# Mixer 1 of a two-block transformer kernel: when its attention starts, and what stands between its steps

## The chip, the cores and the metric

The kernel runs on one core of a Trainium2 chip. The metric is the device time of one launch, in microseconds (us). TensorE does the matrix products, VectorE and ScalarE the elementwise work, GpSimd (POOL in the profile) a few small things, and SyncE issues the loads of weights. A tensor engine bank is one of eight PSUM banks of 512 columns.

## The reference, cut to what matters

The reference is two transformer blocks on 256 tokens of width 1024. The change lies in the first block's second part, the mixer:

```
x = x + 0.5 * gate * swiglu(modulate(x))          # first FFN, "f1"
h = modulate(x, norm_w, shift, scale)             # shift, scale: parts of silu(c) @ w_ada + b_ada
proj = h @ w_in                                   # c_q 256, c_kv 128, k_rope 32, conv 3*512, gates 2*1024
q  = rms_norm(c_q) @ w_uq                         # 8 heads of 64 + 32 (rope)
kv = rms_norm(c_kv) @ w_ukv                       # 8 heads of 64 (key) + 64 (value)
q, k: rms_norm per head, rope on the last 32; k_rope is shared by all heads
o_attn = causal softmax(q k^T * scale) v
o_conv = gate_b * conv3(gate_c * xv)
y = (sum over branches of sigmoid(gates) * (branch @ w_branch)) @ w_out
x = x + gate * y                                  # then the second FFN, "f2", with its own shift and scale
```

The modulation `silu(c) @ w_ada + b_ada` gives 72 columns of 128 values; f2's shift is columns 48 to 55 and its scale columns 56 to 63.

## The kernel before, in words

All activations stand transposed, features on the 128 partitions and 256 tokens along the free dimension. Every fp32 operand is split in two fp32r halves, hi and lo, and a product is three matmuls: hi x hi, hi x lo, lo x hi. A **tile** is one 128 x 128 block of weights, so three matmuls; `Plan.tiles` counts them from the kernel's start, and tile numbers here and below are that count.

Weights come in **units** of up to 2048 columns through a raw buffer of four slots (`load`, SyncE). ScalarE copies a unit to the ring as **hi** (two halves of up to 1024 columns) and VectorE subtracts to get **lo** (two pieces). A unit of modulation weights is two **ada** pieces of VectorE (L209) and needs no hi. A load can be issued when the unit four before it has been used up by its pieces. `take_unit` issues the hi and puts the pieces in a list, `pend`. A piece leaves the list (`piece`) at three kinds of place: `fill()` calls in the code, every 4 tiles when more than two are pending (`went`), and when a unit's first tile is due (`need`: units are taken three ahead, and not more than three pieces may be pending when one is taken). With `self.hold` set the first two do nothing. With `self.apart` set, `take_unit` issues only the first half of hi, and the second half is issued just ahead of the unit's first lo. Unit w33 is the first of mixer 1; w37 holds the queries' weights, w46 those of gates 1.

The order of the work is written out once, in `Plan`, and each engine runs its own steps in that order, strictly one behind the other. In mixer 1 the groups of projections follow `M1_ORDER`: c_q and c_kv (tile 528), conv_in 1 (552), conv_in 0 (568), queries and keys (584), conv_out 0 (604), conv_in 2, conv_in 3, conv_out 2 (652), then gates 1 (668), gates 2 (684), gates 0 (700), and five more groups of gates, each 16 tiles, to tile 796; then the branches and the output projection. Each group has two banks and is evacuated when it is done: for gates, VectorE's `gate_in` twice, then ScalarE's `gate_shift` and `gate_tanh` twice.

Beside them, `in_tiles(n, ...)` starts things n tiles behind tile 604: `heads(0)` and `heads(1)` (scaling and rope of the queries of each half of the tokens, VectorE), `head_keys` (scaling of the keys on VectorE, and a copy of the rope keys to all heads on ScalarE, `heads_kr`), and the **attention**, a generator that is moved on by one step whenever the tile count passes a multiple of 3.5. Its first move does nothing. Its steps are: eight times four transposes of two heads' queries or keys (`turn_heads`, TensorE, L227) with a copy out on ScalarE (`turned_heads`), in banks B0 and B3 by turns, so that the third turn needs the first one's copy done; then in half steps for n = 0, 1, ...: scores of head n (B0 or B3), `masked_1` (VectorE), `exp_1` (ScalarE); turn of P of head n - 2 (bank B1 alone, so it needs the copy out of the turn before it, `turned_1`, ScalarE); the product of P and V for a pair of heads (B7) every other step; and half a step later `between(n)`: `normal_1`, the scaling of head n by its sums (VectorE), and the split of a finished pair into hi and lo (`o_hi_1`, `o_lo_1`).

Before the change the first head turn is at tile 679, the first scores at 707. In ScalarE's order the first two `turned_heads` (tiles 679, 683) stand ahead of the evacuation of gates 1 (684). Two ada pieces (w46's neighbours) stand at tiles 672 and 676, two each at 692 and 708, two at 768.

Of the kernel before, what the change touches and what calls it, by code (L numbers as in the profile page):

```python
# [36 lines left out]
def unit_list():  # L37


    def tile(m, k, f):  # L40
        return (m, k, 128 * f, 128 * (f + 1))

    def chunks(tiles, n=16):
        return [("w", tiles[i:i + n]) for i in range(0, len(tiles), n)]

    def down(m, n, k0=0):
        return [tile(m, k0 + k, f) for f, ks in down_order(n) for k in ks]

    def ada(*ids):
        return ("ada", [("ada", i, 0, 1024) for i in ids])  # L50

    def ada_pairs(first, n):
        return [ada(first + i, first + i + 1) for i in range(0, n, 2)]

    def mix(ws, adas, places):
        out = []
        assert len(adas) == len(places)
        for i, w in enumerate(ws):
            out += [a for a, p in zip(adas, places) if p == i]
            out.append(w)  # L60
        return out

    def ffn_up(m, js):
        return [("w", [t for k in range(8) for t in (tile(m, k, j), tile(m, k, 22 + j))]) for j in js]

    def nat(m, ranges):
        w = sum(b - a for a, b in ranges)
        ks = U // w
        return [("w", [(m, k, a, b) for k in range(k0, k0 + ks) for a, b in ranges]) for k0 in range(0, 8, ks)]

    out = []
    for k in range(8):
        out.append(ada(8 + k, k))
        out.append(("w", [t for j in range(8) for t in (tile("w13a", k, j), tile("w13a", k, 22 + j))]))
    ws = ffn_up("w13a", range(8, 22)) + chunks(down("w2a", 22))
    out += mix(ws, ada_pairs(16, 8) + ada_pairs(32, 8) + ada_pairs(24, 8) + ada_pairs(40, 8), ADA_1)
    ws = [("w", [tile("win", k, f) for k in range(8) for f in range(2)]),
          ("w", [t for k in range(8) for t in (tile("win", k, 2), ("win", k, 384, 416))])]

    def two(m, f, g):  # L80
        return [("w", [t for k in range(8) for t in (tile(m, k, f), tile(m, k, g))])]

    for kind, i in M1_ORDER:
        if kind == "qkv":
            ws += [("w", [("wuq", k, 0, 768) for k in range(2)]), ("w", [("wukv", 0, 0, 1024)])]
        else:
            ws += {"gates": two("wgate", i, 8 + i), "conv_in": two("wconv", i, 8 + i),
                   "conv_out": two("wconv", 4 + i, 5 + i)}[kind]
    ws += chunks([tile("wbr", (k + 4) % 8, f) for f in range(8) for k in range(8)])
    ws += chunks(down("wout", 8))  # L90
    out += mix(ws, ada_pairs(56, 8) + ada_pairs(48, 8), ADA_2)
    ws = ffn_up("w13b", range(22)) + chunks(down("w2b", 22))
    out += mix(ws, ada_pairs(64, 8), ADA_3)
    ws = nat("win2", [(1024, 1536)]) + nat("win2", [(0, 512)]) + nat("win2", [(512, 1024)])
    ws += nat("win2", [(2304, 2816)]) + nat("win2", [(2816, 3072), (2048, 2304)]) + nat("win2", [(1536, 2048)])
    ws += nat("win2", [(3072, 3584)]) + nat("win2", [(3584, 3840)])
    for f in range(8):
        ws += [("w", [tile("win2", k, 30 + f) for k in range(8)] + [tile("woa", k, f) for k in range(8)])]
    ws += chunks([t for f in range(8) for t in [tile("win2", k, 38 + f) for k in range(8)]
                  + [tile("wob", k, f) for k in range(2)]])  # L100
    ws += chunks(down("wout2", 8))
    for half in range(2):
        for f in range(0, 16, 2):
            ws += [("w", [tile("ff1", k, 16 * half + f + i) for k in range(8) for i in range(2)])]
        ws += chunks(down("ff2", 16, 16 * half))
    for a in (0, 512):
        ws += [("w", [("wple", k, a, a + 512) for k in range(2)])] + nat("wpg", [(a, a + 512)])
    return out + ws
# [3 lines left out]
            ("conv_out", 2), ("gates", 1), ("gates", 2), ("gates", 0), ("gates", 3), ("gates", 4), ("gates", 5),  # L112
            ("gates", 6), ("gates", 7)]

ADA_1 = [1, 3, 4, 5, 8, 10, 11, 13, 13, 15, 17, 17, 19, 19, 21, 23]
ADA_2 = [0, 4, 4, 4, 13, 14, 15, 19]
ADA_3 = [5, 6, 9, 17]

PACE, AHEAD, KEEP = 4, 3, 2
# [5 lines left out]
PLE_PARTS = [(0, 0, 512, 2), (1, 0, 512, 2), (0, 512, 1024, 3), (1, 512, 768, 3), (1, 768, 1024, None)]  # L125

STEP_1, STEP_A, STEP_B = 7, 11, 10.5
HEADS_AT, KEYS_AT, ATTENTION_AT = (37, 53), 75, 70
TURN_K, TURN_Q, TURN_B = (20, 10), (13, 7), (3, 10)

COLS = [("b_ada", 72), ("norm_w", 24), ("q_a", 2), ("kv_a", 1), ("wq", 1), ("wk", 1), ("conv", 12), ("b_gate", 16),
# [119 lines left out]
def done(turn, *events):  # L251

    turn.buf.free = events
# [235 lines left out]
class Plan:  # L489
# [296 lines left out]
    def mixer_1(self):  # L786
# [113 lines left out]
        ko = []  # L900
# [3 lines left out]
                kinds[kind](i, lambda k, n=n: ko.append(c_sums()) if (n, k) == sums_at else None)  # L904

        cut = M1_ORDER.index(("qkv", 0))
        run(M1_ORDER[:cut], SUMS_AT)
        ko = ko[0]

        v_b, qn, qr = [B[0].take(), B[3].take()], [B[4].take(), B[5].take()], B[6].take()  # L910
# [33 lines left out]
        def heads(t):  # L944
            b = tmp.take()
            self.add("heads_q", t, b)
            ab = tmp.take(), tmp.take()
            self.add("heads_rope", t, b, ab)
            done(b, ("heads_rope", t))
            done(ab[0], ("t_q", t))  # L950
            done(ab[1], ("t_q", t))

        def head_keys():
            for t in range(2):
                self.add("heads_k", t)
                self.add("heads_kr", t, ko)
            done(ko, ("heads_kr", 0), ("heads_kr", 1))

        def attention():
            for src in range(2):  # L960
                for hp in range(4):
                    yield
                    b = A[hp % 2].take()
                    self.add("turn_heads", src, hp, b)
                    self.add("turned_heads", src, hp, b)
                    done(b, ("turned", src, hp))
            p_b, pt_b = {}, {}

            def scores(h):
                b, s, p = A[h % 2].take(), tmp.take(), tmp.take()  # L970
                self.add("scores_1", h, b)
                self.add("masked_1", h, b, s)
                done(b, ("masked_1", h))
                self.add("exp_1", h, s, p)
                done(s, ("exp_1", h))
                p_b[h] = p

            def turn(h):
                b, p, pt = A[2].take(), p_b.pop(h), tmp.take()
                self.add("turn_1", h, b, p)  # L980
                done(p, ("turn_1", h))
                self.add("turned_1", h, b, pt)
                done(b, ("turned_1", h))
                pt_b[h] = pt

            def pv(h):
                if h % 2:
                    o = B[7].take()
                    pts = [pt_b.pop(h - 1), pt_b.pop(h)]
                    self.add("pv_1", h // 2, o, pts)  # L990
                    for pt in pts:
                        done(pt, ("pv_1", h // 2))
                    o_b.append((h // 2, o))

            def between(n):
                if n < 8:
                    self.add("normal_1", n, p_b[n])
                if o_b:
                    hp, o = o_b.pop()
                    self.add("o_hi_1", hp, o)  # L1000
                    self.fill()
                    self.add("o_lo_1", hp, o)
                    done(o, ("o_1", hp))

            o_b = []
            yield from in_half_steps(scores, turn, pv, between)

        def start():
            self.side, self.every, self.apart = attention(), STEP_1 / 2, True

        self.in_tiles(HEADS_AT[0], lambda: heads(0))
        self.in_tiles(HEADS_AT[1], lambda: heads(1))
        self.in_tiles(KEYS_AT, head_keys)
        self.in_tiles(ATTENTION_AT, start)
        run(M1_ORDER[cut + 1:])
        self.finish_side()
        self.apart = False
        self.add("gcol", 1, 0.5)
        self.add("acol", 2, range(8))
        for f in range(8):  # L1020
            bank = bk.take()
            for k in range(8):
                self.mm(128, "branch", f, k, bank)
            g, q = tmp.take(), tq.take()
            self.add("gated", f, bank, g)
            done(bank, ("gated", f))
            self.add("merged", f, g, q)
            done(g, ("merged", f))
            self.add("merged_hi", f, q)
            self.fill()  # L1030
            self.add("merged_lo", f, q)
            done(q, ("merged_lo", f))
# [349 lines left out]
                stages[i](n - i)  # L1382


def in_half_steps(scores, turn, pv, between):

    for n in range(11):
        yield
        for i, stage in ((0, scores), (2, turn), (3, pv)):
            if 0 <= n - i < 8:  # L1390
                stage(n - i)
        yield
        between(n)
# [2091 lines left out]
```

How the kernel before makes its waits and increments, by code:

```python
    def then_inc(self, signal, n):  # L177
        if self.ins is not None:
# [11 lines left out]
    def wait_ge(self, signal, value):  # L190
        if self.passed.get(signal.name, 0) < value:
            self.passed[signal.name] = value
            if self.e is not None:
                self.e.wait_ge(signal.sem, value)
# [287 lines left out]
    def turn(self, *turns):  # L482
        for t in turns:
            for event in t.before:
                self.e.wait_ge(*self.at(*event))
# [930 lines left out]
    def load(self, i):  # L1417
        m, e = self.m, self.e
        if i >= NR:
            kind, blocks = m.units[i - NR]
            if kind == "ada":
                e.wait_ge(*self.at("ada", blocks[-1][1]))
            else:
                e.wait_ge(*self.at("lo", m.windex[i - NR], 1))
        w = m.widths[i]
        src = m.wts[m.offs[i]:m.offs[i] + 128 * w].rearrange("(p w) -> p w", p=128)
        e.dma_start(m.raw[:, i % NR, 0:w], src).then_inc(*self.up(f"unit{i % NR}_in", ("unit", i), by=16))
# [7 lines left out]
    def load_mask(self):  # L1435
        m, e = self.m, self.e
        e.wait_ge(*self.at("x", "f1", 7))
        e.dma_start(m.reg(34, 256), m.cons2_in[:, 0:256]).then_inc(*self.up("mask_in", ("mask",), by=16))
# [1 line left out]
    def load_tables(self):  # L1440
        m, e = self.m, self.e
        e.wait_ge(*self.at("merged_lo", 7))
        e.dma_start(m.reg(45, 256), m.cons2_in[:, OK2["axc"][0]:OK2["axc"][1]]).then_inc(
            *self.up("cosines_in", ("cosines",), by=16))
        e.dma_start(m.reg(44, 256), m.cons2_in[:, OK2["axs"][0]:OK2["axs"][1]]).then_inc(
```

## Time and profile before

| | us |
|---|---|
| median of 3 runs | 1005.85 |
| lowest, highest | 1005.77, 1007.15 |
| the profiled execution, its own time | 1007.17 |
| its span, first to last instruction | 1005.4 |
| busy: TensorE matmuls, VectorE, ScalarE | 988.8, 771.0, 536.6 |
| mean granted TensorE clock | 0.995 |

A span can be read as slices of time. Granted clock 1.00 is 2.4 GHz, 0.50 is 1.2 GHz. A wait is idle time of an engine that ends when another engine's result comes; a wait for several things is put down to the one that came last. L224 is the line of all matmuls, L227 of all transposes, L197 of all ScalarE operations, so an operation is told by the buffers that it writes and reads.

### The profile page before, as it was taken

The numbers are of one execution on the slowest core, as the hardware profiler recorded it, in microseconds if no ns is written. First come the engines' busy times: TensorE is split into PE (matmuls) and PEld (weight loads), VectorE is DVE, ScalarE is ACT, GpSimd is POOL, SyncE is SP. The second block draws the span as 40 slices with busy tenths as digits, with TensorE's granted clock in tenths as the row PEclk, the third lists the DMA queues.
The fourth block names the chain that finished last, engine by engine and source line by source line (L and its number), as shares of the span: only waits on it lengthen the run. The fifth ranks groups of instructions, "written<-read, shape, count | busy, mean of one in ns | idle before, by whom it ended". The sixth has DMA issues, their size and how long they took to land.

```text
span 1005.4 us, 17440 instructions
## 1 busy us (share of the span) xinstructions
PE 988.8 (98%) x7090; PEld 925.3 (92%) x7090; DVE 771.0 (77%) x1397; ACT 536.6 (53%) x930; POOL 12.0 (1%) x33
## 2 busy tenths in 40 slices
PE   8999999999899999999999999999999999999997
PEld 8999998998898999999988988789999988988896
DVE  6999999879976788685776688547778776677665
ACT  5555554437575565353665446664555554455453
POOL 0000000004000000000000000000000000000000
PEclk9999999999999999999999999999999999999999
DMA  8997998865563555677665435364445555545431
GB/s 334 372 352 260 372 345 327 314 200 211 220 224 130 206 211 184 234 216 230 244 215 201 170 126 209 126 196 126 161 168 181 186 190 187 202 176 177 179 106 42
DMA packets 33678, 213.94 MB, mean 213 GB/s; under 512 B 3773, under 2 KB 6717, under 8 KB 8894
## 3 DMA queue, kind: packets, MB, share of 16 engines
q1 hardware_dynamic: 33310, 211.78, 59.6%
q8 instruction: 56, 0.92, 0.4%
q10 hardware_dynamic: 288, 1.05, 0.3%
q14 instruction: 24, 0.20, 0.1%
HBM read 210.19 MB, written 2.62 MB: 212 GB/s over the span
## 4 chain that ended last, share of the span: by engine, by line
PE 81%; DVE 8%; ACT 4%; DMA 4%; issue 2%; SPq 0%; ACTq 0%; DVEq 0%
PE bank L224 79%; DMA sb_raw<-wts 3%; DVE sb_ring L200 2%; ACT sb_ring L197 2%; PE bank L227 2%; ACT sb_tmp L197 1%; DVE sb_tq L200 1%; DVE sb_junk L209 1%; DVE sb_tmp L200 1%; DMA sb_x<-xt 1%; DMA R<-rows 1%; DVE sb_tmp L206 1%; ACT R L197 0%; DVE R L200 0%; DVE R_512r L200 0%
## 5 line engine op out<-in xcount | busy, mean ns | idle before, releaser
L224 PE MATMUL bank<-sb_h,sb_ring 128*128 128x258 f32 (+2 forms) x3776 | 493.7, 291 | 0.6 <-ACT sb_h L197 0.3
L224 PEld LDWEIGHTS bank<-sb_h,sb_ring 128*128 128x128 f32 x3776 | 472.8, 189 | 14.5 <-issue 2.4
L200 DVE TENSOR_TENSOR sb_ring<-sb_raw,sb_ring 128x1024 fp32r<-128x1024 f32 (+1 forms) x324 | 386.3, 1206 | 10.4 <-ACT sb_ring L197 10.3
L197 ACT ACTIVATE sb_ring<-sb_raw 128x1024 fp32r<-128x1024 f32 (+1 forms) x324 | 320.4, 1037 | 72.0 <-DMA sb_raw<-wts 37.5
L224 PE MATMUL bank<-R_512r,sb_ring 128*128 128x256 f32 (+1 forms) x1608 | 225.7, 301 | 0.0
L224 PEld LDWEIGHTS bank<-R_512r,sb_ring 128*128 128x128 f32 x1608 | 211.5, 188 | 12.0 <-issue 0.5
L224 PE MATMUL bank<-sb_ring,sb_h 128*128 128x512 f32 (+1 forms) x504 | 112.5, 378 | 0.0
L224 PEld LDWEIGHTS bank<-sb_ring,sb_h 128*128 128x128 f32 x504 | 87.4, 188 | 16.6
L209 DVE CUSTOM_DVE_ANT_0 sb_junk<-sb_raw,sb_csil,sb_cols 128x1024 bf16<-128x1024 f32 x72 | 92.3, 1282 | 2.1 <-DMA sb_raw<-wts 0.4
L224 PE MATMUL bank<-R_1024r,sb_ring 128*128 128x512 f32 (+1 forms) x576 | 91.6, 320 | 0.0
L224 PEld LDWEIGHTS bank<-R_1024r,sb_ring 128*128 128x128 f32 x576 | 82.0, 188 | 8.2
L200 DVE TENSOR_TENSOR sb_tq<-bank,sb_rbc 128x256 f32<-128x256 f32 x87 | 33.8, 420 | 52.1 <-ACT sb_zb L197 26.8
L197 ACT ACTIVATE R_512r<-sb_tq 128x256 fp32r<-128x256 f32 x60 | 25.1, 418 | 77.6 <-DVE sb_tq L200 50.6
L197 ACT ACTIVATE sb_tmp<-bank 128x256 f32<-128x256 f32 (+2 forms) x62 | 27.9, 462 | 30.4 <-PE bank L224 27.8
L197 ACT ACTIVATE sb_tmp<-sb_tmp,sb_smx 128x256 f32<-128x256 f32 (+2 forms) x40 | 20.9, 524 | 35.5 <-DVE sb_smx L209 25.3
L206 DVE SCALAR_TENSOR_TENSOR sb_x<-bank,sb_gcol,sb_x 128x256 f32<-128x256 f32 x36 | 17.4, 483 | 27.5 <-PE bank L224 27.0
L197 ACT ACTIVATE sb_h<-sb_x,sb_cols 128x256 fp32r<-128x256 f32 x24 | 14.2, 593 | 37.6 <-DVE sb_x L206 24.0
L200 DVE TENSOR_TENSOR R_512r<-sb_tq,R_512r 128x256 fp32r<-128x256 f32 x60 | 25.2, 420 | 3.9 <-ACT R_512r L197 3.9
L200 DVE TENSOR_TENSOR sb_tmp<-bank,sb_tmp 128x256 f32<-128x256 f32 x32 | 12.4, 425 | 19.1 <-ACT sb_tmp L197 19.0
L197 ACT ACTIVATE sb_tq<-bank 128x256 f32<-128x256 f32 (+1 forms) x35 | 12.9, 367 | 25.7 <-PE bank L224 25.7
L197 ACT ACTIVATE sb_tq<-sb_tq,sb_zb 128x256 f32<-128x256 f32 x26 | 13.3, 510 | 23.6 <-DVE sb_tq L200 23.5
L227 PE MATMUL bank<-sb_con,sb_tmp 128*128 128x128 f32 (+1 forms) x134 | 21.1, 275 | 2.3 <-ACT sb_tmp L197 1.9
(168 smaller groups left out, 576.8 us busy)
## 6 DMA issues: line engine op xcount, KB each, us to landing
sb_raw<-wts SPq DMA_DIRECT2D x193, 1024.0 KB, 4.9
sb_raw<-wts SPq DMA_DIRECT2D x3, 512.0 KB, 3.6
scratch<-R SPq DMA_DIRECT2D x1, 1536.0 KB
sb_x<-xt ACTq DMA_DIRECT2D x2, 512.0 KB, 5.4
R<-scratch SPq DMA_DIRECT2D x2, 508.0 KB, 8.7
sb_raw<-wts SPq DMA_DIRECT2D x1, 768.0 KB, 4.5
sb_raw<-wts SPq DMA_DIRECT2D x1, 640.0 KB, 4.0
R<-scratch SPq DMA_DIRECT2D x2, 258.0 KB, 5.5
```

The lines of the kernel that those rows point to most:

```text
L197: return Issued(self.e and self.e.activation(o, i, func, **kw))
L200: return Issued(self.e and self.e.tensor_tensor(*a))
L206: return Issued(self.e and self.e.scalar_tensor_tensor(*a))
L209: return Issued(self.e and self.e.tensor_tensor_reduce(*a))
L224: return Issued(self.e and self.e.matmul(o, w, m, start=start, stop=stop, skip_group_check=True))
L227: return Issued(self.e and self.e.transpose(o, i, ident))
```

## The change

- The modulation units get other places: columns 56 and 57 go into f1's down projection, the next three units are spread over w35, w36 and w37 (they stood together ahead of w37), and of f2's shift one unit moves from w48 to w52 and one from w52 to w53.
- `apart` holds in conv_in 1 and conv_in 0, and later from tile 660 on (before: from the attention's start).
- `heads(1)` comes 3 tiles earlier, the keys at tile 674 in place of 679, `heads_kr` with each half's queries.
- The attention starts at tile 682 in place of 674; its first turn is at 686 in place of 679, its first scores at 714.
- Behind each scaling one piece is issued, and `hold` keeps all others out, but for those that `need` forces, until head 7's scaling is done. `o_lo_1` comes half a step behind `o_hi_1`.
- `acol(2)` is issued ahead of branch 5 in place of branch 0.

```
-    out += mix(ws, ada_pairs(16, 8) + ada_pairs(32, 8) + ada_pairs(24, 8) + ada_pairs(40, 8), ADA_1)
+    out += mix(ws, ada_pairs(16, 8) + ada_pairs(32, 8) + ada_pairs(24, 8) + ada_pairs(40, 8) + ada_pairs(56, 2), ADA_1)
-    out += mix(ws, ada_pairs(56, 8) + ada_pairs(48, 8), ADA_2)
+    out += mix(ws, ada_pairs(58, 6) + ada_pairs(48, 8), ADA_2)
-ADA_1 = [1, 3, 4, 5, 8, 10, 11, 13, 13, 15, 17, 17, 19, 19, 21, 23]
-ADA_2 = [0, 4, 4, 4, 13, 14, 15, 19]
+ADA_1 = [1, 3, 4, 5, 8, 10, 11, 13, 13, 15, 17, 17, 19, 19, 21, 23, 24]
+ADA_2 = [2, 3, 4, 13, 14, 19, 20]
-HEADS_AT, KEYS_AT, ATTENTION_AT = (37, 53), 75, 70
+HEADS_AT, HALVES_AT, KEYS_AT, ATTENTION_AT = (37, 50), 56, 70, 78
...
+        self.apart = True
         run(M1_ORDER[:cut], SUMS_AT)
+        self.apart = False
...
             done(ab[1], ("t_q", t))
+            self.add("heads_kr", t, ko)
         def head_keys():
             for t in range(2):
                 self.add("heads_k", t)
-                self.add("heads_kr", t, ko)
...
                 p_b[h] = p
+                self.hold = True
...
             def between(n):
                 if n < 8:
                     self.add("normal_1", n, p_b[n])
+                    self.piece()
+                else:
+                    self.hold = False
                 if o_b:
                     hp, o = o_b.pop()
                     self.add("o_hi_1", hp, o)
-                    self.fill()
+                    o_rest.append((hp, o))
+
+            def rest():
+                if o_rest:
+                    hp, o = o_rest.pop()
                     self.add("o_lo_1", hp, o)
                     done(o, ("o_1", hp))
...
+            yield from in_half_steps(scores, rest, turn, pv, between)
+            yield
+            rest()
+
+        def in_halves():
+            self.apart = True
         def start():
-            self.side, self.every, self.apart = attention(), STEP_1 / 2, True
+            self.side, self.every = attention(), STEP_1 / 2
+        self.in_tiles(HALVES_AT, in_halves)
...
-        self.add("acol", 2, range(8))
         for f in range(8):
+            if f == 5:
+                self.add("acol", 2, range(8))
...
     for n in range(11):
         yield
-        for i, stage in ((0, scores), (2, turn), (3, pv)):
+        if n < 8:
+            scores(n)
+        rest()
+        for i, stage in ((2, turn), (3, pv)):
```

## Rows read from the trace of the kernel before

**Rows 1.** The page: busy us (share of the span) and instructions of each engine.

```profile
PE 988.8 (98%) x7090; PEld 925.3 (92%) x7090; DVE 771.0 (77%) x1397; ACT 536.6 (53%) x930; POOL 12.0 (1%) x33
```

**Rows 2.** TensorE's waits, 220 to 345 us: who waited for whom, total, times, longest.

```profile
PE bank L227 <- ACT sb_tmp L197: 1.6, 2, 1.4
PE bank L224 <- ACT sb_tq L197: 1.1, 1, 1.1
...
PE bank L227 <- DVE sb_tmp L203: 0.2, 1, 0.2
```

**Rows 3.** TensorE in order of time: start, us, instructions, idle time before them.

```profile
239.16 27.11 PE L224 MATMUL bank<-sb_h,sb_ring 128*128 128x258 f32 x225
266.11 0.76 PE L227 MATMUL bank<-sb_con,R 128*96 128x128 f32 x4
...
272.79 0.64 PE L227 MATMUL bank<-sb_con,R 128*96 128x128 f32 x4 [2.97 <-ACT R L197]
...
277.78 0.60 PE L227 MATMUL bank<-sb_con,R 128*96 128x128 f32 x4
...
281.20 0.60 PE L227 MATMUL bank<-sb_con,R 128*96 128x128 f32 x4
...
287.78 0.82 PE L224 MATMUL bank<-R,R 96*128 96x256 f32 x4
...
316.17 0.55 PE L227 MATMUL bank<-sb_con,sb_tmp 128*128 128x128 f32 x3 [1.40 <-ACT sb_tmp L197]
...
320.07 0.49 PE L227 MATMUL bank<-sb_con,sb_tmp 128*128 128x128 f32 x3
```

**Rows 4.** Four stretches: length, engines' busy us, granted clock, DMA share, GB/s.

```profile
226.00:264.00 38.00, 36.70 (x284) 35.34 (x283) 36.53 (x77) 25.85 (x52) 11.59 (x28) 1.00 0.59 213
...
274.00:277.00 3.00, 3.00 (x17) 2.97 (x16) 3.00 (x5) 2.09 (x5) 0.00 (x0) 0.54 0.93 366
277.00:280.00 3.00, 3.00 (x24) 3.00 (x24) 2.85 (x5) 1.93 (x4) 0.00 (x0) 0.89 0.68 188
...
330.00:450.00 120.00, 120.00 (x999) 119.52 (x998) 94.66 (x166) 63.67 (x118) 0.00 (x0) 1.00 0.62 209
```

**Rows 5.** VectorE in order of time, columns as in rows 3.

```profile
266.20 0.75 DVE L200 TENSOR_TENSOR sb_tmp<-bank,sb_rbc 128x256 f32<-128x256 f32 x2
...
270.59 1.28 DVE L209 CUSTOM_DVE_ANT_0 sb_junk<-sb_raw,sb_csil,sb_cols 128x1024 bf16<-128x1024 f32 x1
...
274.33 0.75 DVE L200 TENSOR_TENSOR sb_tq<-bank,sb_rbc 128x256 f32<-128x256 f32 x2
...
308.12 0.41 DVE L209 CUSTOM_DVE_ANT_0 sb_tmp<-bank,R 128x256 f32<-128x256 f32 x1
...
308.67 1.22 DVE L200 TENSOR_TENSOR sb_ring<-sb_raw,sb_ring 128x1024 fp32r<-128x1024 f32 x1
```

**Rows 6.** ScalarE in order of time, columns as in rows 3.

```profile
218.50 1.58 ACT L197 ACTIVATE sb_ring<-sb_raw 128x768 fp32r<-128x768 f32 x2 [10.01 <-DMA sb_raw<-wts]
...
231.63 0.21 ACT L197 ACTIVATE sb_tq<-bank 128x72 f32<-128x72 f32 x1
...
271.45 0.70 ACT L197 ACTIVATE R<-sb_tq 128x256 f32<-128x256 f32 x2
...
274.84 0.17 ACT L197 ACTIVATE sb_zb<-bank 128x1 f32<-128x1 f32 x1 [1.54 <-DVE sb_tq L200]
...
276.06 1.04 ACT L197 ACTIVATE sb_ring<-sb_raw 128x1024 fp32r<-128x1024 f32 x1
277.00 1.24 ACT L197 ACTIVATE R<-bank,sb_wqk 96x512 f32<-96x512 f32 x2
...
305.77 0.51 ACT L197 ACTIVATE sb_tmp<-sb_tmp,sb_smx 128x256 f32<-128x256 f32 x1 [1.91 <-DVE sb_smx L209]
...
306.67 0.46 ACT L197 ACTIVATE sb_tmp<-bank 128x384 f32<-128x384 f32 x1
```

**Rows 7.** The page's list of DMA issues: count, KB each, us to landing.

```profile
sb_raw<-wts SPq DMA_DIRECT2D x1, 768.0 KB, 4.5
```

More of the change, by code:

```diff
@@ L1000, in between @@
                     self.add("o_hi_1", hp, o)
-                    self.fill()
+                    o_rest.append((hp, o))
+            def rest():
+                if o_rest:
+                    hp, o = o_rest.pop()
                     self.add("o_lo_1", hp, o)
                     done(o, ("o_1", hp))
-            o_b = []
-            yield from in_half_steps(scores, turn, pv, between)
+            o_b, o_rest = [], []
+            yield from in_half_steps(scores, rest, turn, pv, between)
[3 more added lines that the diff above has]
+            self.apart = True
         def start():
-            self.side, self.every, self.apart = attention(), STEP_1 / 2, True
+            self.side, self.every = attention(), STEP_1 / 2
         self.in_tiles(HEADS_AT[0], lambda: heads(0))
         self.in_tiles(HEADS_AT[1], lambda: heads(1))
+        self.in_tiles(HALVES_AT, in_halves)
         self.in_tiles(KEYS_AT, head_keys)
@@ L1382, in in_steps, with in_half_steps @@
                 stages[i](n - i)
-def in_half_steps(scores, turn, pv, between):
+def in_half_steps(scores, rest, turn, pv, between):
     for n in range(11):
         yield
-        for i, stage in ((0, scores), (2, turn), (3, pv)):
+        if n < 8:
+            scores(n)
+        rest()
+        for i, stage in ((2, turn), (3, pv)):
             if 0 <= n - i < 8:
```

## The prediction

> **What bounds the kernel now.** I read the page's busy shares first, then TensorE's waits, then TensorE's instructions in order of time, the busy time of all engines by stretch, and last VectorE's and ScalarE's own order, to see who is late. TensorE is busy for 988.8 of 1005.4 us [rows 1], so a change in the order of work can only win back idle time and lowered clock. Of its 16.6 us of idle time mixer 1 holds 5.9 [rows 2, 3]: 0.2 us in conv_in 0, 1.1 us ahead of the queries (at 231 us), 2.97 us ahead of the third head turn, and 1.6 us at two turns of P, 1.40 of it at that for head 6. Behind the 2.97 us the granted clock is 0.54 and 0.89 for two stretches of 3 us [rows 4], that is the lower level (1.2 GHz) for some 3.3 us. From 272.79 to 277.78, TensorE does 4 + 12 + 4 + 9 matrix instructions [rows 3]; the same at full clock takes the 3.42 us from there to 281.20, so the low clock cost 4.99 - 3.42 = 1.57 us. With the idle time mixer 1 loses 5.9 + 1.6 = 7.5 us.
>
> VectorE is what stands behind it. In 226 to 264 us it is busy for 36.53 of 38 us, and ScalarE for 25.85 [rows 4]. TensorE passed 75 tiles in 27.11 us [rows 3], 0.36 us a tile, so it was at tile 668 (counted from the kernel's start) near 262 us; VectorE takes up that tile's results at 266.2 us and those of gates 1 (tile 684) only at 274.33 [rows 5]. It is 4 us late, then more.
>
> Matmul busy says TensorE is the fullest engine here, 36.70 of 38 us against 36.53 [rows 4]. The Trainium skill, Perfetto Trace Analysis, section Identifying the Most-Contended Engine, takes the weight loads' share for TensorE and plain occupancy for VectorE, and says to work on the fullest: by that it is VectorE, 36.53 against 35.34 us. Going by the busy share, giving TensorE work ahead of the attention removes its waits, some 1000 us; going by the Trainium skill's measure nothing is won while VectorE's list stays as long, near 1006 us or above. By that rule VectorE is the bound here, and the trace, with VectorE 4 us late, agrees.
>
> **The change part by part.**
>
> *Modulation rows in other places, second halves later in conv_in 1 and 0.* Two pieces go to f1's down projection, and four of those that stood in one bunch at tile 544 to 552 are spread ahead of it; none is added (a piece is 1.28 us of VectorE, [rows 5]). Before, ScalarE stood 10.01 us waiting for the load of the queries' weights, because that load is issued only when a raw slot comes free behind the bunch; it then did that hi for 1.58 us and only after it the token factors [rows 6]. After, that load follows the unit of w35, done near 209 us, and lands (4.5 us for 768 KB, [rows 7]) near 213.6, so the factors are there when the c projections end, near 218, and not at 220.2. VectorE's chain there runs 2 us earlier; most of that only becomes waiting for conv_in 0. What counts: the queries waited 1.1 us for a bank that ScalarE freed at 231.8 [rows 2, 6], behind a hi of two halves. Now it is free before 229, and the 0.2 us in conv_in 0 go too. Gain for TensorE 1.3 us; bounds 0 and 1.35. VectorE cannot follow wholly: in 226 to 264 us it idles 1.5 us in all [rows 4], and only what lies ahead of its unbroken run from 239 us on can be won; I take 0.9 of the 1.5.
>
> *Rope keys copied in heads().* Two copies of 0.35 us [rows 6] leave the place ahead of the first turned heads and go where ScalarE has 12 us idle of 38 [rows 4]: off the path, and -0.7 us at the new place. heads_k comes 12 tiles and more before the first key turn: nothing waits for it, before or after. The acol moved to f = 5 is one operation on eight columns, less than the 0.41 us of half a masked score [rows 5]: nothing, from -0.4 to 0.4.
>
> *Attention 8 tiles later.* This is the term that decides. The steps fall on multiples of 3.5 tiles, so the first turn moves from tile 679 to 686. Gates 1 ends at tile 684, between the two. In the old order the first two turned heads stood ahead of gates 1's results in ScalarE's queue; in the new order they stand behind them. That queue then reads: conv_hi, one half of hi, [gate shift and tanh, twice, which wait for VectorE's gate_in], second half of hi, first half of the next hi, first turned head. The third turn (tile 693) uses the first one's bank and needs that last item.
>
> - VectorE: gate_in starts at 274.33 - 0.9 = 273.4. Its list up to there is the same (two modulation rows from 270.59, heads_k twice, gate_in, [rows 5]).
> - ScalarE: before, from gate_in at 274.33 to turned heads at 277.00 took 2.67 us with one half of hi in it [rows 5, 6]; a half is 277.00 - 276.06 = 0.94. With two halves 3.6, so the first turned head starts at 277.0 and TensorE goes on 0.7 us later (half of the pair's 1.24 us and the release): 277.7.
> - TensorE: tile 604 at 239.16 - 1.3 = 237.86, then 82 tiles of 0.36 to 267.3; from the first turn to the third is (272.79 - 2.97) - 266.11 = 3.71 [rows 3], so it stands ready at 271.0.
>
> The stall is 6.7 us in place of 2.97. Bounds: 5.5, if VectorE gains another 1.1, and 7.5, if it gains nothing. The clock drops after it: at least once as before. 1.6 us; bounds 0.8 and 2.5, as the idle time is longer than any before it in this trace and I have no row for its length.
>
> At 277.7 TensorE is at tile 693 with two turns done. Before, it was there at 277.78 with four done, and its low clock behind it. A turn is (3.42 - 7 x 0.36) / 2 = 0.45, and from 281.20 to 287.78 lie 14 tiles, two turns and scores(0): 0.6 to 0.7. So scores(0), now at tile 714, starts at 277.7 + 21 x 0.36 + 6 turns (2.6) + 1.6 = 289.4; before, tile 714 came at 287.78 with scores(0) done, 287.1 without. Position: +2.3 us.
>
>
> *One piece behind each scaling.* From tile 714 on I walked ScalarE's and VectorE's queues in order with these increments: scores 0.85 until VectorE can start, masked 0.55 (308.12 to 308.67), exp 0.9, turned P 0.4, scaling 0.66 (306.67 to 308.12 without gate_in), lo 1.14, gate_in 0.68, gate's two shifts and tanh 1.22, half of hi 0.94 [rows 5, 6]. Exactly eight pieces follow, all lo; two modulation rows (2.6 us) leave this stretch for w52 and w53. But the piece stands directly between a scaling and the next gate_in and masked. Thus at tile 732: scaling(2) 299.5, lo to 301.3, gate_in to 302.0, tanh and hi on ScalarE to 304.0, exp(3), turned P(1) at 305.3; turn(2) was ready at 303.5 and waits 1.8 us for the one bank. Again, turn(4) waits 1.2 us at 313.2. The others have room. 3.0 us; bounds 0 and 4. Before: 1.6 by [rows 2], and some 0.9 us that the walk does not resolve. At tile 770 I get 321.6 with turn(6) and a PV pair (1.15 us) still due, so 322.75 against the 320.07 at which TensorE started turn(7) before: +2.7 us.
>
> After the attention nothing is late: o_lo(3) is issued at tile 791 and needed at 803, 4.3 us, and from 330 to 450 TensorE never waits [rows 4]. The two modulation rows that move behind it find VectorE with idle time, as the first ones moved to f1.
>
> **Sum.** Span 1005.4 + 2.7 = 1008.1; the profiled execution took 1007.17, 1.8 more than its span, and lies 1.3 above the median of the three runs, 1005.85. I add 2.7 to that median: 1008.5 us.
>
> **The rivals.**
> - *VectorE is in time and the stall goes (the other side).* Of 7.5 us lost only the 3.0 of my walk would remain: 1005.85 - 4.5 = 1001.4. It decides at one point: gate_in of gates 1 must start 4.3 us (3.6 + 0.7) before tile 693 is reached, at 266.7; I have 273.4. For it: the modulation rows bunched ahead of 552 are gone, and VectorE is 2 us ahead there. Against: it waits for conv_in 0 then, and has hardly any idle time for 35 us behind it [rows 4]. 0.16.
> - *The stall stays, the attention flows.* If the walk is wrong by one queue place, its waits go and two modulation rows are off its path: 1008.5 - 3.0 = 1005.5. For it: before, exp ran after masked at once in most steps; against: the 1.40 us before came in just this way, with exp 1.91 us late [rows 5, 6]. 0.25.
> - *Nothing moves:* the needs of each unit force the pieces back to where they were, and the stall is given back: 1005.9. 0.06.
> - *The low clock lasts longer* or comes again at the 1.8 us wait: 1.6 + 0.5 more: 1010.6. 0.08.
>
> **Numbers.** My forecast has 0.45, its own range 1007 to 1010.3. About 0.2% (2 us) is what a measurement can tell here from no change. Slower by more: most of my case and the low clock, 0.48; within: the flowing attention, nothing moves, the lower edge of mine, 0.35; faster: 0.17. Range 1002.8 to 1010.6: it leaves out most of the fast rival and the top of the slow one.
>
> **What would show it.** Right: a wait of TensorE of some 6.7 us ahead of the third head turn, released by ScalarE's turned heads, with gate tanh and two hi halves ahead of it; clock at the lower level behind it; no wait ahead of the queries, and ScalarE's 10 us wait for the load gone. Wrong: that wait under 3 us, or turned heads ahead of gate tanh; or turns of P that never wait. The wrong step would then be VectorE's backlog or the walk.

## The result

| | before | after |
|---|---|---|
| median, us | 1005.53 (6 runs, 1004.97 to 1007.15) | 1009.12 (6 runs, 1008.12 to 1011.47) |
| profiled execution, its span | 1007.17, 1005.4 | 1009.41, 1007.6 |
| mixer 1, c_q's first tile to the first branch | 205.05 to 330.75 = 125.70 | 203.88 to 333.82 = 129.94 |

The ratio is 1.0035, 95% interval 1.0025 to 1.0045: the change costs 3.6 us. The forecast was 1008.5. Two executions of the same code may reach mixer 1 some us apart (below), so what follows goes by the length of mixer 1: 4.24 us longer. From the first branch to f2's down projection it is 0.82 us shorter (330.75 to 506.33 before, 333.82 to 508.58 after; a wait of 0.2 us for weights in f2's up projection is gone, the other 0.6 isn't placed), which leaves 3.42.

TensorE's waits after, 220 to 345 us (who waited for whom, total, times, longest), against [rows 2]:

```profile
PE bank L227 <- ACT R L197: 6.6, 1, 6.6
PE bank L227 <- ACT sb_tmp L197: 1.7, 1, 1.7
```

The wait for the queries' bank (1.1) is gone; the one at the third head turn has grown from 2.97 to 6.62. TensorE after, in order of time, against [rows 3]:

```profile
229.38 7.15 PE L224 MATMUL bank<-sb_ring,R_512r 128*128 128x512 f32 x36
236.36 29.92 PE L224 MATMUL bank<-sb_h,sb_ring 128*128 128x258 f32 x246
266.13 0.60 PE L227 MATMUL bank<-sb_con,R 128*96 128x128 f32 x4
...
268.35 1.34 PE L224 MATMUL bank<-sb_h,sb_ring 128*128 128x258 f32 x9
276.31 1.09 PE L227 MATMUL bank<-sb_con,R 128*96 128x128 f32 x4 [6.62 <-ACT R L197]
...
281.89 0.60 PE L227 MATMUL bank<-sb_con,R 128*96 128x128 f32 x4
...
288.70 0.81 PE L224 MATMUL bank<-R,R 96*128 96x256 f32 x4
...
302.28 0.82 PE L224 MATMUL bank<-R,R 96*128 96x256 f32 x4
304.82 0.83 PE L227 MATMUL bank<-sb_con,sb_tmp 128*128 128x128 f32 x3 [1.72 <-ACT sb_tmp L197]
...
310.26 0.82 PE L224 MATMUL bank<-R,R 96*128 96x256 f32 x4
```

And three stretches after (length, engines' busy us, granted clock, DMA share, GB/s), against [rows 4]; the second lies inside the stall, the third behind it:

```profile
226.00:264.00 38.00, 38.00 (x295) 36.89 (x295) 34.34 (x74) 23.90 (x47) 12.23 (x28) 1.00 0.54 195
...
273.00:276.00 3.00, 0.00 (x0) 0.00 (x0) 2.08 (x3) 2.97 (x6) 0.00 (x0) 0.70 1.02 333
276.00:279.00 3.00, 2.69 (x13) 2.67 (x14) 2.49 (x4) 1.51 (x3) 0.00 (x0) 0.50 0.73 208
```

From the third turn to the fifth TensorE took 281.89 - 276.31 = 5.58 us, at full clock 3.42: the low level cost 2.16. It came again behind the 1.72 us wait at the turn of P for head 2: from scores(4) to scores(5), 302.28 to 310.26, 7.98 us; the same work without wait or low clock takes 4.50 (313.76 to 318.26), so 1.76 us of it are clock. ScalarE after, in order of time, against [rows 6]:

```profile
212.35 1.58 ACT L197 ACTIVATE sb_ring<-sb_raw 128x768 fp32r<-128x768 f32 x2 [5.04 <-DMA sb_raw<-wts]
...
267.32 1.04 ACT L197 ACTIVATE sb_ring<-sb_raw 128x1024 fp32r<-128x1024 f32 x1
272.48 0.17 ACT L197 ACTIVATE sb_zb<-bank 128x1 f32<-128x1 f32 x1 [4.11 <-DVE sb_tq L200]
...
273.69 1.99 ACT L197 ACTIVATE sb_ring<-sb_raw 128x1024 fp32r<-128x1024 f32 x2
275.59 1.24 ACT L197 ACTIVATE R<-bank,sb_wqk 96x512 f32<-96x512 f32 x2
```

The first head turn has been in its bank since 266.7, and ScalarE stands idle for 4.11 us with that copy ready to be done: its next item is gates 1's, and gates 1 waits for VectorE. VectorE itself then has time:

```profile
271.97 0.75 DVE L200 TENSOR_TENSOR sb_tq<-bank,sb_rbc 128x256 f32<-128x256 f32 x2
...
282.16 0.75 DVE L200 TENSOR_TENSOR sb_tq<-bank,sb_rbc 128x256 f32<-128x256 f32 x2 [3.63 <-PE bank L224]
```

It idles 3.63 us for results of TensorE, which had stood still while ScalarE waited for VectorE.

### The profile page after: what moved, and what is told of

The parts are those of the page before. It is cut to its first block, busy times and chain, and to the rows that moved or that the text cites. A ratio compares the mean times of both kernels' runs of the same rounds, so it can differ in the third digit from the quotient of the medians.

```text
span 1007.6 us, 17440 instructions
## 1 busy us (share of the span) xinstructions
PE 989.4 (98%) x7090; PEld 925.7 (92%) x7090; DVE 770.7 (76%) x1397; ACT 537.0 (53%) x930; POOL 12.6 (1%) x33
## 4 chain that ended last, share of the span: by engine, by line
PE 88%; DVE 7%; DMA 2%; ACT 2%; issue 1%; ACTq 0%; DVEq 0%
PE bank L224 86%; DVE sb_ring L200 2%; PE bank L227 2%; DMA sb_raw<-wts 1%; DVE sb_junk L209 1%; ACT sb_ring L197 1%; DVE sb_tmp L206 1%; DVE sb_tmp L200 1%; DMA sb_x<-xt 1%; ACT sb_tmp L197 0%; DVE R L200 0%; DVE sb_st_v L212 0%; ACT R L197 0%; DVE R L206 0%; DVE sb_tq L200 0%
## 5 line engine op out<-in xcount | busy, mean ns | idle before, releaser
L197 ACT ACTIVATE sb_zb<-bank 128x1 f32<-128x1 f32 x76 | 9.6, 158 | 26.7 <-DVE sb_tq L200 16.4
```

What stands on the lines that cost most here:

```text
L197: return Issued(self.e and self.e.activation(o, i, func, **kw))
```

## The experiments

Every one was timed against the kernel before, whose median was 1004.9 to 1005.6 in these sets. M is the length of mixer 1 in the profiled execution (before 125.70, after 129.94). Each M is from one trace; how far it would repeat is known only from waits that an edit leaves alone, and these do repeat (6.62 at the third head turn in after and e6; 1.41 to 1.42 in e1, e7, e9 and e11). Units are counted here over the whole list, modulation units included: 75, 77 and 78 are w46, w47 and w48, the weights of gates 3, 4 and 5. (Those of gates 1 are w43, and not w46 as the kernel's description has it.)

| | base, edit | median | ratio, interval | M |
|---|---|---|---|---|
| e1 | after, start 70 | 1007.81 | 1.0026, 1.0014 to 1.0038 | 128.25 |
| e2 | before, start 78 | 1008.32 | 1.0036, 1.0024 to 1.0048 | 128.07 |
| e3 | after, two modulation units away | 1008.69 | 1.0028, 1.0014 to 1.0042 | 125.99 |
| e4 | before, front's units alone | 1003.74 | 0.9990, 0.9980 to 1.0000 | 124.63 |
| e5 | after, gates 1's ScalarE half later | 1008.04 | 1.0020, 1.0011 to 1.0030 | 128.79 |
| e6 | after, no piece rule | 1008.33 | 1.0027, 1.0016 to 1.0037 | 128.98 |
| e7 | e6, start 70 | 1006.76 | 1.0011, 1.0002 to 1.0021 | 127.37 |
| e8 | e5, copy of unit 77 later | 1005.82 | 0.9997, 0.9988 to 1.0005 | 126.04 |
| e9 | e7, both later | 1000.77 | 0.9954, 0.9941 to 0.9966 | 121.00 |
| e10 | e9, copy of unit 75 later | 1000.31 | 0.9950, 0.9938 to 0.9963 | 120.68 |
| e11 | e9 with the piece rule | 1002.48 | 0.9974, 0.9962 to 0.9986 | 122.98 |
| e12 | e8, gates 2 and unit 78 later | 1001.97 | 0.9963, 0.9949 to 0.9977 | 120.97 |

**Which part of the change costs.** e1 takes the start back, e2 makes only the start later.

```
e1 (after)   -..., ATTENTION_AT = (37, 50), 56, 70, 78
             +..., ATTENTION_AT = (37, 50), 56, 70, 70
e2 (before)  -HEADS_AT, KEYS_AT, ATTENTION_AT = (37, 53), 75, 70
             +HEADS_AT, KEYS_AT, ATTENTION_AT = (37, 53), 75, 78
```

> The changed kernel with the attention's start alone put back to 70 tiles, so the first head turn is at tile 679 again, ahead of gates 1's evacuation at 684; all else of the change stays. Theory 1 (VectorE is late, ScalarE's queue passes it on): the 6.6 us wait ahead of the third turn shrinks to about 2 us (hi half 1.0, turned heads 0.7), but the fifth turn (tile 693) then waits for turned heads (0,2) behind gates 1, some 3 to 4 us, since gate_in of gates 1 still starts near 272 us. Total idle near 5.5 us, but in two parts; time 1006.5 to 1008. Theory 2 (only the place of the start matters, VectorE has room): no wait over 1 us at any head turn and no low clock, time 1001 to 1003.

> The kernel before with the attention's start alone put from 70 to 78 tiles. Theory 1: the third turn, now at tile 693, waits for the first turned heads behind gates 1's evacuation, some 5.4 us (gate_in 274.3, turned heads 277.0, TensorE ready at 272.3), the low clock costs about 2 us behind it; with the old order of pieces in the attention the later waits stay as before. 1007.5 to 1009.5. Theory 2 (the later start is harmless, what costs is the one piece behind each scaling): 1005 to 1006.

The third and fifth head turns of e1, and the third of e2:

```profile
268.39 0.64 PE L227 MATMUL bank<-sb_con,R 128*96 128x128 f32 x4 [1.42 <-ACT R L197]
...
275.71 1.09 PE L227 MATMUL bank<-sb_con,R 128*96 128x128 f32 x4 [3.71 <-ACT R L197]
```

```profile
278.87 1.09 PE L227 MATMUL bank<-sb_con,R 128*96 128x128 f32 x4 [5.46 <-ACT R L197]
```

In e2 one number, 70 to 78, makes the third turn wait 5.46 in place of 2.97, and the median 3.5 us longer (1004.87 to 1008.32), as much as the whole change. By M it is 2.37 of the 4.24; its five executions may have reached mixer 1 late, as the profiled one did, which isn't shown for the others. In e1 the stall goes to the fifth turn, since two turns stand ahead of gates 1 in ScalarE's order and the third turned head behind it.

e3 and e4 part the modulation rows. e3 takes four ada pieces out of VectorE's list ahead of and behind gates 1's end and puts them into the branches; e4 gives the kernel before the change's front part (three units spread, one pair to f1, halves of hi apart in conv_in 1 and 0).

```
e3 (after)   -ADA_2 = [2, 3, 4, 13, 14, 19, 20]
             +ADA_2 = [2, 3, 4, 19, 20, 21, 22]
e4 (before)  +... + ada_pairs(56, 2), ADA_1)  and  ADA_1 = [..., 23, 24]
             ... (ada_pairs(58, 6) in place of ada_pairs(56, 8) for ADA_2)
             -ADA_2 = [0, 4, 4, 4, 13, 14, 15, 19]
             +ADA_2 = [2, 3, 4, 13, 14, 15, 19]
             +        self.apart = True
                      run(M1_ORDER[:cut], SUMS_AT)
             +        self.apart = False
```

> The changed kernel with the two units of f2's shift rows that stand ahead of the attention (four pieces at tiles 672, 676, 692, 696) moved behind it, to w52 and w53, and the other two to w54 and w55; work of VectorE is only moved. Theory 1: gate_in of gates 1 starts 2.5 us earlier (about 269.4 against 271.97), the wait ahead of the third turn falls from 6.6 to about 4.1 us, one for one, and the low clock costs the same or less: 1005.5 to 1007. Theory 2 (ScalarE's own list, not VectorE, holds the turned heads back): wait and time unchanged, 1009.

> The kernel before with only the front of the change: modulation columns 56 and 57 in f1, the next three units at w35, w36, w37, and half hi in conv_in 1 and conv_in 0. The attention and its pieces as before. Theory 1: the 1.1 us wait ahead of the queries and the 0.2 us in conv_in 0 go, VectorE gains 1.2, so the third turn's wait grows by 0.3: 1.2 us faster than before, 1004.3. Theory 2 (VectorE sets the time, so what TensorE gains ahead of it is given back whole at the third turn): the wait there grows by 1.3 or more, no gain, 1005.5.

```profile
275.22 0.64 PE L227 MATMUL bank<-sb_con,R 128*96 128x128 f32 x4 [3.27 <-ACT R L197]
...
362.21 18.42 PE L224 MATMUL bank<-R_512r,sb_ring 128*128 128x256 f32 x153 [1.97 <-DVE R_512r L200]
```

Those are e3's: the stall fell from 6.62 to 3.27 and M by 3.95, more than forecast, since the edit did two things: gate_in started 2.4 us earlier in the mixer, and one of the two copies came to stand behind the first turned head (2.67 us from gate_in to it, in place of 3.62). But the pieces then made VectorE late further on, and the output projection waited 1.97 us. By the trace some 1.7 us should be left; the median shows 0.4 of it (1008.69, forecast 1005.5 to 1007), from executions that lie between 1005.1 and 1011.4. The rest isn't explained. e4 has M 1.07 shorter than before: the queries no longer wait, and the third turn waits 2.98 as before. So the front is worth 1.1 us by itself, by M and by the medians (1004.87, 1003.74), though the interval reaches 1.0000.

**The piece rule.** e6 is after without it, e7 the same with start 70.

```
e6, e7 (after)   -                self.hold = True
                 -                    self.piece()
                 (o_lo_1 directly behind fill() again; in e7 also ATTENTION_AT 70)
```

> The changed kernel without its rule of one piece of other work behind each scaling and none elsewhere (the pieces come again by the count of tiles, and o_lo stands directly behind o_hi); the start 8 tiles later and all else stay. Nothing is left out. My prediction's step (the rule adds waits of 1.8 and 1.2 at turns of P, where before had one of 1.4): theory 1, the rule is worth less than 1.5 us either way, since in both kernels one turn of P waits 1.4 to 1.8; what it takes with it here is the second stretch of low clock (about 1.3 us) if the wait then falls elsewhere: 1007.3 to 1009.3, the likeliest 1008.2; the third head turn still waits 6 to 7. Rival: the rule is the main cost of the change (waits and clock together 3 us or more): 1006 or less. Other rival: the rule helps, VectorE coming to exp's data earlier: 1010 or more.

> As the last kernel (no rule of one piece behind each scaling), and the attention started at 70 tiles as before: what is left of the change is the front's modulation rows, the split of the second high halves, the keys' rope with the queries, the second heads 3 tiles earlier, heads_k at 70. Nothing is left out. With the two others it closes a square: start 70 or 78, rule or none. If start and rule add up: the changed kernel at 78 with the rule 1009.1, at 70 with the rule 1007.8, so this one is the last kernel less 1.3, some 1006.9 (1006 to 1008). Rival, that they interact (started at 70 with the rule, P's turns wait 0.88, 0.78 and 0.27; by the count of tiles one wait of 1.4): 1004 to 1005.9. Waits on ScalarE's evacuation of 1.4 and 3.7 at the third and fifth head turns by both.

With e1 they close a square of M: rule and 78 129.94, rule and 70 128.25, none and 78 128.98, none and 70 127.37. The rule costs 0.9 to 1.0 us at either start, the later start 1.6 to 1.7 with the rule or without: they add up. In e6 the third head turn waits 6.62 as well, and one turn of P, now head 4's, waits 1.76. From e4 to e7 M grows by 2.74 with the start at 70 in both; the fifth head turn, which had no wait in e4, waits 3.73 in e7. Between them lie the heads and keys, and the half of unit 75's copy that `apart` puts behind gates 1; none was tried alone. The two traces suggest the half: from gate_in to the turned head behind gates 1 are 2.68 us in e4 and 3.63 in e7, so the fifth turn comes 0.75 us later in the mixer, and the low clock (2.54 us) then lies behind it, where in e4 it (1.58) was over by that turn.

So M grows from before to after in four steps: the front -1.07, heads, keys and `apart` +2.74, the later start +1.61, the piece rule +0.96. The later start isn't the largest of them. In another order the steps would differ: the start costs 2.37 in the kernel before (e2).

**What the stall is made of.** e5 leaves every engine's work as it is and moves four ScalarE instructions: `gate_shift` and `gate_tanh` of gates 1 come 14 tiles later, behind the first four turned heads. e8 moves the copy `hi(77)` too.

```
e5, e8       def scalar_half():      # gate_shift, gate_tanh and their releases
                 ...
             if f == 1:
                 self.in_tiles(14, scalar_half)
             ...                       # other groups: scalar_half() at once
e8 only      if i == 77:
                 self.in_tiles(14, lambda: self.add("hi", i, w, (0,)))
             ...                       # other units as before
```

> The changed kernel, with ScalarE's half of the evacuation of gates 1 (gate_shift, gate_tanh) put 14 tiles later in the written order, behind the evacuations of the first four head turns; VectorE's half (gate_in) stays where it is. Nothing is left out. The same work for every engine, another order in one queue. Theory 1 (the 6.62 us stall at the third head turn is ScalarE's queue: the evacuation of the first turn, whose bank has been full since 266.7, stands behind gates 1, which waits for VectorE until 272): the third turn finds its bank free (wait under 0.5, from 6.62), the clock stays high there, and what is late next is VectorE itself, at gates 0 (the low half of its weights and gate_in, about 272 to 274 where TensorE comes at 273): one wait of 0.5 to 3 us. Net gain on the change 4 to 7 us: 1002 to 1005. Theory 2 (VectorE's total work is the bound, and the order of ScalarE's queue only says where the stall shows): the wait moves behind the fourth turn or into gates 0 with about the same size, 5 to 6 us, and the time stays at 1007.5 to 1009.

> The run with the turned heads first (ScalarE's half of gates 1 put 14 tiles later), and with it the copy of the next unit's first high half (unit 77, sb_ring<-sb_raw) put 14 tiles later too: that copy stood between the gates and the first turned head and waited 3.75 us for its load, which landed at 272.9. Nothing is left out. Theory 1 (the stall is ScalarE's queue: whatever waits ahead of the first turned head, for VectorE or for a load, holds TensorE; two such stood there one behind the other, so that moving one gave only 1.5 us): ScalarE evacuates the first turn at 268.2, the third turn waits under 0.3, the clock stays high up to 273; then gates 0 needs the low half of its unit, ready at 273.7 (wait 0.5 to 1), and the next copy (unit 78, its load out of a slot free at 271.9, so here at about 276 to 277) stands ahead of the sixth turned head: up to 1.5 us at the eighth turn. Of the 5.07 wait and some 2 of low clock 3.5 to 6 go: 1002 to 1005, the likeliest 1003.5, which is faster than before. Theory 2 (the loads and VectorE bound this stretch as a whole; the order only says where it shows): the same 5 us at the fifth to eighth turn or at gates 0, 1007 to 1008.5.

The third turn of e5, and ScalarE ahead of it:

```profile
274.60 1.09 PE L227 MATMUL bank<-sb_con,R 128*96 128x128 f32 x4 [5.07 <-ACT R L197]
```

```profile
267.17 1.99 ACT L197 ACTIVATE sb_ring<-sb_raw 128x1024 fp32r<-128x1024 f32 x2
272.92 1.06 ACT L197 ACTIVATE sb_ring<-sb_raw 128x1024 fp32r<-128x1024 f32 x1 [3.75 <-DMA sb_raw<-wts]
273.88 1.24 ACT L197 ACTIVATE R<-bank,sb_wqk 96x512 f32<-96x512 f32 x2
```

My forecast for e5 failed: the wait fell by 1.55 and not by 6. Taking the gates away uncovered a second item ahead of the turned heads, a copy of weights not needed for two groups more, whose load landed only at 272.9. By its time, 1008.04, e5 would have spoken for theory 2. In e8 both are gone:

```profile
271.77 0.64 PE L227 MATMUL bank<-sb_con,R 128*96 128x128 f32 x4 [0.26 <-ACT R L197]
...
283.61 1.09 PE L227 MATMUL bank<-sb_con,R 128*96 128x128 f32 x4 [2.95 <-ACT R L197]
```

The third turn waits 0.26 us. The eighth then waits 2.95, about twice what I gave it, with another 2.75 us of low clock behind it: its bank's turned head stands behind gates 2 and two copies. So e8 by itself decides nothing: its time, 1005.82, lies between what the two theories had (to 1005, and from 1007), and of the 7.4 us of wait and low clock that went at the third turn 5.7 came back at the eighth. If that is the same fault further on, moving gates 2 and the next copy too (e12) must end it; e9 makes e8's two edits in e7.

```
e12 (e8)     -if i == 77:              +if i in (77, 78):     # 78: 12 tiles later
             -if f == 1:               +if f in (1, 2):       # gates 2: 12 tiles later
```

> The run with start 70 and no piece rule, with the same two things put 14 tiles later (ScalarE's half of gates 1 and the copy of unit 77). Nothing is left out. That run waits 1.41 at the third head turn (behind work in ScalarE's queue that stays there), 3.73 at the fifth (behind the gates and the copy), 0.41 at the first, and 1.41 at a turn of P; low clock follows the fifth's. Theory 1: the fifth's wait goes and the low clock with it (some 1.8), the others stay, and up to 1.5 us come back at the last head turns, behind the copy of unit 78: 1006.8 less 3 to 5.5 = 1001.5 to 1003.8, the likeliest 1002.5, the fastest of all. Theory 2: the 3.7 us come back whole at a later turn or at gates 0: 1006 to 1007.5.

> The run with start 78 and the rule, ScalarE's half of gates 1 and the copy of unit 77 put later, and here ScalarE's half of gates 2 and the copy of unit 78 put 12 tiles later as well, behind the last turned head. Nothing is left out. That run still waits 2.95 at the eighth head turn, for the turned head that stands behind gates 2 (idle 2.04 until VectorE's gate_in) and two copies (281.00 to 282.89), and the clock is low behind it. Theory 1 (ScalarE's order is the whole stall of the start 8 tiles later): the eighth turn waits under 0.3, the clock stays high, 2.95 and 1.5 to 2 us go: 1005.8 to 1001 to 1001.7; scores(0) at about 282 to 283. Theory 2 (a start 8 tiles later can't be had: the wait shows next at gates 3, for its banks or weights, or at scores(0)): 1003.5 to 1005.5.

TensorE's waits, 203 to 345 us, of e9, and then of e12:

```profile
PE bank L227 <- ACT R L197: 1.4, 1, 1.4
PE bank L227 <- ACT sb_tmp L197: 1.4, 1, 1.4
PE bank L227 <- DVE R L200: 0.4, 1, 0.4
```

```profile
PE bank L227 <- ACT sb_tmp L197: 2.5, 2, 1.7
PE bank L227 <- ACT R L197: 0.3, 1, 0.3
```

These two decide for theory 1. e9: the fifth turn's 3.73 us of e7 are gone whole, and none came back at gates 0 or at a later turn; M is 6.37 shorter than e7's. Of that 3.73 is the wait, and 2.54 the low clock behind it (e7 took 5.96 us from the fifth turn to the seventh, in place of 3.42). The median fell by 6.0, to 1000.77, under the 1001.5 to 1003.8 that I gave it. e12: with the later start and the rule both kept, M is 120.97, 8.97 shorter than after, by moves in ScalarE's order alone; by the medians of the two sets it is 7.15 (1009.12, 1001.97). The wait at the eighth turn is gone with the low clock behind it; turn(2) waits 1.72 there, where e8 had 1.24, and the time is 0.3 above my forecast's upper end (1001.7).

**Two more.** e10 puts the copy of unit 75 behind the first turned head; e11 is e9 with the piece rule.

```
e10 (e9)     -if i == 77:              +if i in (75, 77):     # 75: 12 tiles later
e11          e1 with e8's two edits
```

> The fastest version so far (start 70, no piece rule, ScalarE's half of gates 1 and the copy of unit 77 put 14 tiles later), and the copy of unit 75's first high half put 12 tiles later too, behind the first turned head. Nothing is left out. That copy (1.04 us, ScalarE busy 269.69 to 270.63) stands ahead of the first turned head, and the third head turn waits 1.42. Theory 1 (ScalarE's queue): the first turned head starts at about 269.7 in place of 270.63, the third turn waits about 0.5, the time falls by 0.9: 1000.8 to 999.9 (999.3 to 1000.6). Theory 2 (what the stretch waits for is VectorE or a load, and the wait comes back elsewhere): 1000.6 to 1001.2, with a wait of 0.5 to 1 at gates 0 or at a later head turn.

> The version with start 70, ScalarE's half of gates 1 and the copy of unit 77 put 14 tiles later, but with the change's rule of one piece behind each scaling. Nothing is left out. What the rule costs by itself where no stall and no low clock stand ahead of it: from the square (78: 1009.1 with, 1008.3 without; 70: 1007.8 with, 1006.8 without) 0.8 to 1.1 us: 1001.6 to 1001.9, with three short waits at turns of P (0.9, 0.8, 0.3, together 1.9) in place of one of 1.42. By the waits alone it is 0.5: 1001.3. Rival, that the rule's cost was a trace of the low clock after the stall: 1000.4 to 1001.0. Other rival: it costs 2 or more, 1002.8 up.

e10's three waits in the same stretch, and its engines' busy time around the head turns:

```profile
PE bank L227 <- ACT sb_tmp L197: 1.4, 1, 1.4
PE bank L227 <- ACT R L197: 0.5, 1, 0.5
PE bank L227 <- DVE R L200: 0.4, 1, 0.4
```

```profile
264.00:276.00 12.00, 11.53 (x99) 11.32 (x98) 11.96 (x20) 8.24 (x17) 0.00 (x0) 1.00 0.59 203
```

The third turn's wait fell as forecast, 1.42 to 0.47, but M only by 0.32 of the 0.95. A part came back where the view of TensorE's matrix instructions doesn't show it, at a weight load of scores(1), 276 to 284 us:

```profile
PEld bank L224 <- ACT R L197: 0.3, 1, 0.3
```

The eighth turned head, which it needs, now stands behind two copies. Counted from mixer 1's start, scores(0) comes 0.93 us earlier than in e9 and scores(1) 0.65; the rest goes in small steps up to the end of the attention. By the medians e9 and e10 can't be told apart. e10 has the lowest: 0.5% under before, 0.85% under after. e11: M is 1.98 longer than e9's, so the rule costs 1.7 to 2.0 us with nothing stalled ahead of it, more than the 0.9 that I gave it from the square; its four waits at turns of P (0.88, 0.84, 0.77, 0.27) add up to 2.76 against 1.42.

## Why the prediction held, point by point

- *The queries' wait* (1.3): gone. From c_q's first tile to the queries 27.05 us before, 25.50 after: 1.55.
- *VectorE's gain* (0.9): gate_in starts 68.09 us behind mixer 1's start, before 69.28: 1.19. The load of the queries' weights came as forecast, counted from mixer 1's start (8.5 us), but ScalarE's wait for it isn't gone, as I had written: 5.04 us of the 10.01 remain, and hold up nothing.
- *The attention 8 tiles later.* From gate_in to the first turned head 3.62 us (3.6), from there to TensorE 0.72 (0.7), stall 6.62 (6.7). Rows that show a queue's order gave this to a tenth.
- *The clock* (1.6): 2.16 at the stall, inside the bounds; and 1.76 a second time, behind the 1.72 us wait at turn(2). That second time is the term that was mis-sized: it stood in a rival with a chance of 0.08 and 0.5 us.
- *One piece behind each scaling*: turn(2) waits 1.72 (1.8), for the copy of head 1's turned P, which starts at 304.30, behind exp(3) at 303.43 and a copy of weights at 302.48: the queue as walked. turn(4) was to wait 1.2 and does not. In e12, where the clock stays high behind turn(2)'s 1.72, turn(4) waits 0.77: so the low clock most likely hid it in after; argued from two traces, not tried.
- *Sum*: 2.7 forecast; 4.24 in mixer 1, less 0.82 behind it, is 3.42. The rows of stalls and clock (6.62 + 1.72 + 2.16 + 1.76 = 12.3 after, 7.5 before) make 4.8; 0.6 of that isn't placed. At scores(0) the forecast was 0.5 us short, which is the stall's clock (2.16 for 1.6); by turn(6) it was 0.9 shorter still, for the greater part the 1.76 of clock that wasn't in the sum, less the 1.2 of turn(4) that was and didn't come.
- *Luck*: 1008.5 lies 0.6 from the median, closer than the working deserves. The missed clock was offset by a wait that didn't come and by 0.82 us won behind the mixer that no term has.
- *Rope keys, acol, rows behind the attention*: no wait shows at any of them.

The rivals: VectorE was not in time (gate_in at 271.97, TensorE ready at the third turn at 269.69), so the fast rival's condition never arose and its price wasn't tried. Of the flowing attention half came: turn(4) doesn't wait, turn(2) does. The clock did come a second time, at 1.76 us where that rival had 0.5. What the prediction had too narrow is the reason. It said that the stall ends when VectorE's late list reaches gate_in, and that giving TensorE room therefore needs a shorter list. e5, e8, e9 and e12 together show that VectorE's lateness need not stop the head turns: it is the *place* of the gates and of a copy in ScalarE's queue that passed it on. I had that queue written out, item by item, and read it only as a sum of durations; I had no row for the load behind the second copy, since before, the gates' wait hid it.

Row and page part here. In e10 VectorE is busy for 11.96 of the 12 us around the head turns (264 to 276; 11.89 before), while weight loads take 11.32 (8.59); TensorE's one wait in that stretch is 0.47 us, and the time is 5.1 us less with VectorE's total unchanged (770.1 us, before 771.0, [rows 1]). The Trainium skill, Perfetto Trace Analysis, section Identifying the Most-Contended Engine, says to work on the fullest engine, by which I wrote that nothing is won while VectorE's list stays as long; the measurement decides against that.

## What to carry to other kernels

- Where one engine stands idle for another, look at what stands *behind* the waiting instruction in its queue: if a result that a third engine needs is ready there, move it ahead. That took 9 us out of the mixer here, 7 of the median, with no instruction more or less (after to e12), where moving VectorE's work itself (e3) was given back in great part.
- A copy issued early for weights needed late is not free: it holds its queue until its load lands. Two such holds, one behind the other, hide each other; taking one away and seeing little change does not clear the other.
- Before a start time is moved, list for each engine which items it now passes. The eight tiles here cost what they did with the end of a group between; with the order mended (e12) the later start shows no such wait. Other distances weren't tried.

## What the runs showed of the hardware

- The granted clock after a wait of TensorE does not follow the wait's length alone. Cost of the low level (1.2 GHz) behind the wait, from rows of the same work: 2.95 us of idle time 2.75 (e8), 2.97 us 1.57 (before), 2.98 us 1.58 (e4), 3.27 us 1.60 (e3), 3.71 us 2.32 (e1), 3.73 us 2.54 (e7), 5.07 us 2.59 (e5), 5.46 us 1.66 (e2), 6.62 us 2.16 (after) and 1.30 (e6). Three waits within 0.03 us of each other cost 1.6 twice and 2.75 once. In before, e3 and e4 the granted clock falls only behind the wait, in the others already inside it (0.70 and 0.50 in 273 to 276 us in after and e6), so part of it falls on idle time.
- Waits of 1.72 to 1.76 us at a turn of P were followed by low clock in after, e3, e5 and e6 and not in e2 and e12 (1.00 throughout); waits of 1.37 to 1.42 at one (before, e4, e7, e9, e10) never. These are e6, behind its 1.76, and e12, around its 1.72:

```profile
312.00:315.00 3.00, 3.00 (x19) 2.71 (x16) 1.85 (x6) 2.67 (x7) 0.00 (x0) 0.62 0.61 254
315.00:318.00 3.00, 3.00 (x21) 2.94 (x21) 0.86 (x3) 0.03 (x1) 0.00 (x0) 0.81 0.02 5
```

```profile
297.00:300.00 3.00, 2.08 (x17) 1.60 (x18) 2.40 (x8) 0.87 (x5) 0.00 (x0) 1.00 0.00 0
300.00:303.00 3.00, 3.00 (x26) 2.94 (x25) 1.95 (x5) 2.70 (x7) 0.00 (x0) 1.00 0.91 279
```

The first two stretches are e6's, the others e12's. What tells them apart stays open.
- Executions with the same code ahead of mixer 1 reach it at different times: before at 205.05 and e2 at 206.22, e7 at 203.41 and e9 at 206.26 us. The first 20 us already differ: a block of 22 matrix instructions near 10 us takes 2.70 us in e10, at a granted clock of 1.00, and 5.04 in e9, at 0.50. The difference is as large as the effects studied, so where a median and a stage's length disagree, as for e2, e3 and e12, I go by the length; each is from one trace.
